# A hybrid decoder trunk: the state space scan by blocks of four tokens instead of token by token, with its tables made apart from the mixer

## The reference, cut to what matters

```python
for l in range(DEPTH):
    h = rmsnorm(x, norm_mix[l])
    u, sq, sk, sv, dq, dk, dv, gate_logits = split(h @ w_in[l])
    y_ssm = gelu(s5_ssm(u, ...)); glu_a, glu_b = split(y_ssm @ w_glu[l]); y_ssm = glu_a * sigmoid(glu_b)
    y_sb = stick_breaking_attention(sq, sk, sv)      # 8 heads of 64
    y_da = differential_attention(dq, dk, dv, lam)   # 4 heads, partial rotary, subln
    x = x + sum_n(sigmoid(gate_n) * (y_n @ w_branch[l, n])) @ w_out[l]
    x = x + cross_attention(rmsnorm(x), rmsnorm(mem)) @ w_xo[l]
    x = x + square(relu(rmsnorm(x) @ w_up[l])) @ w_down[l]
out = rmsnorm(x)

def s5_ssm(u, ...):            # 32 groups of 16 channels, 64 complex states in each
    lam_bar = exp(lam * exp(log_dt)); b_bar = (lam_bar - 1) / lam * b
    s[t] = lam_bar * s[t-1] + b_bar @ u[t]
    return real(c @ s[t]) + d * u[t]
```

## Time and profile before

| | |
|---|---|
| median of 3 runs | 1209.06 us (1208.31 to 1209.67) |
| profiled execution | 1207.81 us, span 1206.1 us, TensorE clock 0.935 |
| busy in the span | PE 1090.8, PEld 963.5, DVE 876.0, ACT 565.9, POOL 302.8 us |
| read from HBM | 168.11 MB |

### The profile page before, as it was taken

How to read it: one execution, slowest core, us unless ns; L and a number is a source line. 1 busy time by engine, 2 the same in 40 slices (tenths; PEclk the granted TensorE clock), 3 DMA queues, 4 the chain that set the end, 5 groups by cost and what they waited for, 6 DMA issues and landing times. The chain is left out here.

```text
span 1206.1 us, 18306 instructions
## 1 busy us (share of the span) xinstructions
PE 1090.8 (90%) x6855; PEld 963.5 (80%) x6855; DVE 876.0 (73%) x1236; ACT 565.9 (47%) x874; POOL 302.8 (25%) x362
## 2 busy tenths in 40 slices
PE   3997898879999799999979798988899987999996
PEld 3985677769989688998869566767699976998995
DVE  5769999986877475555567899999778756555553
ACT  4643433236565454444444443332475654544442
POOL 0496775510000000000008868653100000000000
PEclk7997988889999989999979988987899998999998
DMA  7652323323554445565646422422255543555550
GB/s 254 184 156 68 109 71 105 100 76 132 184 182 145 128 136 185 187 191 192 186 117 180 122 70 71 124 86 78 98 175 181 177 131 99 183 191 190 184 186 35
DMA packets 138076, 170.34 MB, mean 141 GB/s; under 512 B 18043, under 2 KB 96005, under 8 KB 137989
## 3 DMA queue, kind: packets, MB, share of 16 engines
q1 hardware_dynamic: 137572, 168.91, 44.3%
q10 hardware_dynamic: 416, 0.26, 0.1%
HBM read 168.11 MB, written 1.05 MB: 140 GB/s over the span
## 5 line engine op out<-in xcount | busy, mean ns | idle before, releaser
L1124 DVE TENSOR_TENSOR s_w_lo<-s_raw,s_w_hi 128x1024 fp32r<-128x1024 f32 x312 | 419.5, 1369 | 165.5 <-ACT s_w_hi L742 161.0
L742 ACT ACTIVATE s_w_hi<-s_raw 128x1024 fp32r<-128x1024 f32 x312 | 320.9, 1054 | 186.7 <-PE p_T L1586 114.6
L1584 PE MATMUL p_T<-s_hT_hi,s_w_hi 128*128 128x256 f32 x1152 | 341.9, 297 | 14.2 <-DVE s_hT_lo L1184 14.2
L1585 PE MATMUL p_T<-s_hT_lo,s_w_hi 128*128 128x256 f32 x1152 | 336.8, 292 | 0.0
L1586 PE MATMUL p_T<-s_hT_hi,s_w_lo 128*128 128x256 f32 x1152 | 336.4, 292 | 0.0
L1584 PEld LDWEIGHTS p_T<-s_hT_hi,s_w_hi 128*128 128x128 f32 x1152 | 233.0, 202 | 26.5 <-issue 26.0
L1585 PEld LDWEIGHTS p_T<-s_hT_lo,s_w_hi 128*128 128x128 f32 x1152 | 233.2, 202 | 0.5
L1586 PEld LDWEIGHTS p_T<-s_hT_hi,s_w_lo 128*128 128x128 f32 x1152 | 232.1, 201 | 0.0
L1584 PE MATMUL p_A<-s_w_hi,s_bT_hi 128*128 128x512 f32 x320 | 124.9, 390 | 2.4 <-DVE s_bT_lo L1124 2.4
L1585 PE MATMUL p_A<-s_w_lo,s_bT_hi 128*128 128x512 f32 x320 | 124.7, 390 | 0.0
L1586 PE MATMUL p_A<-s_w_hi,s_bT_lo 128*128 128x512 f32 x320 | 124.5, 389 | 0.0
(11 more groups left out here) (249 smaller groups left out, 1824.4 us busy)
## 6 DMA issues: line engine op xcount, KB each, us to landing
s_raw<-in_w_in SPq DMA_DIRECT2D x104, 512.0 KB, 3.6
s_raw<-in_w_up SPq DMA_DIRECT2D x64, 512.0 KB, 3.7
s_raw<-in_w_down SPq DMA_DIRECT2D x64, 512.0 KB, 3.6
s_raw<-in_w_branch SPq DMA_DIRECT2D x24, 512.0 KB, 3.6
s_raw<-in_w_out SPq DMA_DIRECT2D x16, 512.0 KB, 3.6
s_raw<-in_w_xkv SPq DMA_DIRECT2D x16, 512.0 KB, 3.5
s_raw<-in_ssm_w_glu SPq DMA_DIRECT2D x8, 512.0 KB, 3.5
s_raw<-in_w_xq SPq DMA_DIRECT2D x8, 512.0 KB, 3.5
```

The lines of the kernel that those rows point to most:

```text
L742: return nc.scalar.activation(o, i, f, **kw)
L1124: return V.tensor_tensor(o, i0, i1, op)
L1584: mm(o, lhi, rhi, start=first, stop=False, **kw)
L1585: mm(o, lhi, rlo, start=False, stop=False, **kw)
```

## The change

The scan goes over blocks of 4 tokens. With the input laid out by blocks (`uB`, filled by `blocks`), `bt` folds four tokens into one state update, `ct` reads the state at the block's start for four tokens, and a block Toeplitz matrix `kt` (with the skip term in it) gives what the four tokens do to each other. Per tile the scan has 64 places instead of 256, and there are four steps instead of eight. The tables are larger: `p_angle`, `p_cos` (ScalarE, VectorE), `tables` and `zero_b` (GpSimd: powers, a 64-place rotation table, zeroing), `p_cv`, `p_b0`, `p_bv` (VectorE), `p_ct`, `p_k`, `p_bt` (TensorE, emptied by ScalarE). Layer 0 makes them at units 0 to 6 and begins the scan at unit 7, layer 1's are made at units 50 to 70 of layer 0 and its scan begins at unit 8; `gelu` follows at unit 12 and 13. The rings shrink, the work on `mem` before layer 0 goes, and `mem` is loaded again in each layer.

```diff
-LO, HI = 10, 6
+LO, HI = 6, 4
...
+        after(u["angle"], "p_angle", tgt)
+        after(u["cos"], "p_cos", tgt)
+        after(u["ct"], "p_ct", tgt)
...
+        pre(0, dict(angle=0, cos=0, ct=1, cv=(1, 2), b0=3, bv=(3, 4), k=(4, 4), bt=(4, 5, 5, 6)))
+        first = 7
+        pre(1, dict(angle=up0 + 6, cos=up0 + 7, ct=up0 + 9, cv=(up0 + 11, up0 + 13), b0=up0 + 15,
+                    bv=(up0 + 16, up0 + 18), k=(up0 + 18, up0 + 20),
+                    bt=(up0 + 21, up0 + 22, up0 + 23, up0 + 24)))
+        after(up0 + 4, "p_spread", 1)
+        after(up0 + 5, "p_params", 1)
...
+    else:
+        first = 8
+    for kb in range(4):
+        after(first + kb, "ssm_in", kb)
+        after(first + 1 + kb, "ssm_out", kb)
+    after(first + 5, "gelu")
...
-    for i in range(SSM_STEPS):
-        after(7 + 2 * i, "ssm_in", i)
-        after(8 + 2 * i, "ssm_rot", i)
-        after(min(10 + 2 * i, 23), "ssm_out", i)
-    after(23, "gelu")
...
-    after(33, "memg")
+    after(33, "mem_turn", 0)
+    after(33, "mem_turn", 1)
+    after(34, "mem_turn", 2)
+    after(34, "mem_turn", 3)
```

The copy of u, run by VectorE for unit 0 and by ScalarE for unit 1, has 16 instructions:

```diff
+        def blocks(copy, b, key, st):
...
+            for q in range(4):
+                for j in range(BL):
+                    i = 8 * key[1] + q
+                    ins = copy(uB[32 * j:32 * j + 32, i:i + 5:4, :], src[32 * q:32 * q + 32, :, :, j])
```

GpSimd's program, in order, and the first waits of `p_cv` and `p_b0` on VectorE:

```diff
+                if l == 0:
+                    tables(st, 0, 0)
+                    zero_b(st, 0, 0)
...
+                if l + 1 < DEPTH:
+                    pool.wait_ge(*st.mine())
+                    tables(st, l + 1, l)
+                    zero_b(st, l + 1, l)
...
+                def p_cv(t, r):
+
+                    if r == 0:
+                        dve.wait_ge(*st.at(*freed(l, "X1", ("p_ct", t))))
+                        dve.wait_ge(*st.at(pow_ready, t + 1))
...
+                def p_b0(t):
+
+                    dve.wait_ge(*st.at(mat_landed, 6 * (t + 1)))
+                    dve.wait_ge(*st.at(pow_ready, t + 1))
+                    dve.wait_ge(*st.at(b_zeroed, t + 1))
```

The new scan step on VectorE (four tiles of 64 places; `io` is the bank, r the real and the imaginary part), and TensorE's two products:

```diff
+                    tt(v[:, :, :, 1:NB], io, turned(0)).then_inc(*st.mid())
+                    tt(t0[:, :, :, 1:NB], io, turned(1)).then_inc(*st.sig(*freed(l, b, s)))
                     dve.wait_ge(*st.mine())
...
+                        V.tensor_tensor_scan(vf, dect[:, sl, :].rearrange("p i m -> p (i m)"), vf, 0.0, ALU.mult, ALU.add)\
...
+                        for r in range(2):
+                            for q in range(4):
+                                c, i = r * T + q * NB, 4 * kb + q
+                                ins = mm(bank[b][:, c + 1:c + NB], bt[:, r, i, :], uB[:, i, 0:NB - 1],
+                                         start=True, stop=True)
...
                             for r in range(2):
...
+                                mm(bank[b][:, c:c + NB], ct[:, r, i, :], st_y[:, r, i * NB:i * NB + NB],
+                                   start=(r == 0), stop=False)
+                            ins = mm(bank[b][:, c:c + NB], kt[:, i, :], uB[:, i, :], start=False, stop=True)
```

More of the change, by code:

```diff
@@ L268, in stage_banks @@
         [["A0", "A1", "A3", "A2"][s[1]]] if s[0] == "xa_p" else [])
+NORMS = ["mix", "cross", "mlp"]
+NORM_SEQ = [(l, n) for l in range(DEPTH) for n in ("mix", "mem", "cross", "mlp") if n != "mem" or l == 0]
 KEYS = [None] * NU
@@ L424, in hybrid_trunk @@
         lo_made = signal("w_lo_made", NC)
-        lo_made_pool = signal("w_lo_made_pool", sum(2 * (pool_cols(u) > 0) for u in range(NU)))
         chunk_done = signal("chunk_done", NC)
[L427 to L433, removed]
+        prm_landed = counted("prm_landed", 9 * DEPTH, step=16)
@@ L559, in _ @@
                     load_chunk(l * NC + c)
[L560 to L570, removed]
@@ new lines, in zero_b @@
+            def zero_b(st, t, l):
+                pool.wait_ge(*st.at(h_ready, KD // 2 if l == t else 3 * KD // 2))
+                for h in range(2):
+                    rows, o = slice(STATES * h, STATES * h + STATES), GC * (1 - h)
+                    pool.wait_ge(*st.mine())
+                    nc.gpsimd.memset(bN0[rows, :, :, o:o + GC], 0.0).then_inc(*st.mid())
+                    for r in range(2):
+                        ins = nc.gpsimd.memset(bN[rows, r, :, :, o:o + GC], 0.0)
+                        ins.then_inc(*st.sig(b_zeroed, t + 1)) if h and r else ins.then_inc(*st.mid())
@@ new lines, in p_k @@
+                def p_k(s):
+                    t, n = s[1:]
+                    b = stage_banks(s)[0]
+                    act.wait_ge(*st.at(*full_at(l, b, s)))
+                    src = bank[b][:, :].rearrange("p (i c) -> p i c", c=P)
+                    for j in range(BL):
+                        rows = slice(32 * j, 32 * j + 32)
+                        ins = fn(kt[rows, 4 * n:4 * n + 4, 32 * j:P], src[0:32, :, 0:P - 32 * j])
+                        ins.then_inc(*st.sig(*freed(l, b, s))) if j == BL - 1 else ins.then_inc(*st.mid())
@@ L1568, in turn_rows @@
                 return ins
-            pe.wait_ge(mem_landed, 16)
-            for j, b in enumerate(TURN_BANKS):
-                turn_rows(b, j, xn).then_inc(pre_pe, 1)
-            pe.wait_ge(pre_dve, 4)
-            for t in range(NT):
-                ins = mm(bank["A1"][:, t * P:t * P + P], ones[:, :], dg[t], start=True, stop=True)
-            ins.then_inc(pre_pe, 1)
-            pe.wait_ge(pre_dve, 9)
             pe.wait_ge(x_landed, 16)
@@ L1682, in stage @@
-                        ins.then_inc(*st.sig(full["A1"]))
+                            ins = mm(bank[b][:, t * P:t * P + P], ones[:, :], dg[t], start=True, stop=True)
+                        ins.then_inc(*st.sig(full[b]))
                     elif kind == "turn_x":
                         for t in range(NT):
-                            pe.wait_ge(*st.at(*norm_input(s[1], s[2], t)))
+                            pe.wait_ge(*st.at(*norm_input(l, s[1], s[2], t)))
                         for j, b in enumerate(stage_banks(s)):
-                            pe.wait_ge(*st.at(*before(b, s)))
+                            pe.wait_ge(*st.at(*before(l, b, s)))
```

1087 lines of the change are left out of this document (590 added, 497 removed).

## The result

The changed kernel takes **1268.49 us** (median of 4 runs, 1266.31 to 1273.96) where the kernel before took 1208.68 beside it: a ratio of 1.0503, 95% interval 1.0468 to 1.0538. It is 5% slower. The forecast was 1212, in a range of 1178 to 1242. The profiled execution has a span of 1264.3 us, 58.2 more than before.

What follows compares the result with a forecast made beforehand. It took TensorE to bound the MLP and VectorE's late head chains, with lost clock, the mixers; terms -5 + 57 - 39 - 43 + 19 + 12 + 5 - 2 = +4 on 1207.8 gave 1212 us, range 1178 to 1242.

Steps and rivals of the forecast that it cites:

- Layer 0's tables: Layer 0's first units: waiting on one chain through GpSimd to p_k leaves TensorE idle about 25 us; +57 (45 to 68).
- Layer 1's tables in the MLP: Layer 0's MLP: TensorE's added table work of 17.5 us, the other engines' hidden in slack, plus a lump; +19.
- +1.5 for that (0 to +12): Layer 0's MLP: allowance for p_b0 at unit 61 waiting on GpSimd, 45 us behind the cosines.
- 41 to 55: GpSimd's chain from the cosines through tables and zero_b: estimated us before p_b0 may start, 46 taken.
- a rival at 0.14, with 1237: Layer 0's MLP: late b_zeroed holds VectorE before p_b0 with low parts behind; GpSimd at 55, +25, 1237; chance 0.14.
- mild at small sizes: GpSimd and VectorE contention, as argued for the rival of cheap narrow products and sufficient ring: 1188, chance 0.27.
- The mixers, -39 and -43: Units 6 to 25, layers 0 and 1: VectorE relieved, TensorE waits only for gelu and the last heads; bounds +-12 each.
- Smaller rings, +6 in each layer: After the mixers: preparation serves a unit one sooner, so units 35, 37 and 40 wait; bounds 0 to +10.
- a stall costs twice: TensorE: idle time is followed by half clock; after 4.17 us idle a product took 1.65 us instead of 0.91.
- Memory again: +2.7: Layer 0, the memory redone per layer: 16 transposes at 0.13 and a broadcast; +2.1 in layer 1.
- The start: Before unit 0: the memory's load, statistics and transposes go, so VectorE's run begins earlier; -5, bounds -3 to -8.
- The rival without a hole: Layer 0's first units: p_b0 ready by unit 4, 25 us less and more, 1180; chance 0.05.

Runs made afterwards that it cites:

- e1: The changed kernel with GpSimd's six memsets of the B tables placed ahead of its tables in both layers: 1219.55 us.
- e2: The changed kernel with layer 1's p_b0, p_bv, p_k and p_bt six units later in layer 0's MLP: 1242.59 us.
- e7: The changed kernel with SyncE issuing layer 1's 15 small loads, and waiting for the MLP's norm, four chunks later: 1267.18 us.
- e3: The changed kernel with each gelu half's 16 activations replaced by one of 128x512, without the token permutation: 1250.06 us.
- e4: The kernel before with rings of 6 and 4 chunks for 10 and 6, and preparation two chunks less ahead: 1227.78 us.
- e9: The changed kernel with layer 1's scan from unit 2 in place of unit 8: 1278.20 us.
- e10: Layer 1's scan from unit 2, against e5 with e7's edit and unit 35's chunks prepared ahead of the memory's work at unit 33: 1202.30 us.
- e5: e1 with one gelu activation per half into a scratch tile, and permuting copies later on VectorE and ScalarE: 1198.02 us.

## Why the prediction was wrong

It forecast +4 and got +60 (58.2 in the profile). Three terms fail, each on the side of what the change adds; they carry 26, 15 and 7 of the 54 by which the stages miss. Layer 0's tables are 5 more.

*Layer 1's tables in the MLP, +19, measured +45.4.* The 17.5 of TensorE's work was nearly right: without the waits it is about 20 (45.4 less 20.8 by e1 and e2, less 4.8 by e7's profile). What failed is "+1.5 for that (0 to +12)". The step before it was right in its mechanism and wrong in one number: GpSimd needs "41 to 55", taken from rows of 128x16 at 0.2 us, and took 64.9. I had it as a rival at 0.14, with 1237, and the mechanism is that rival's; it came on top of all other terms, and 10 us late became 22. Beside GpSimd's chain in the MLP, VectorE makes the low parts of a unit every 5.7 us or so. I let contention cost VectorE's low parts 1.1 us and gave GpSimd's operations 5 us in all; a 16-element operation goes from 0.2 to 0.8 to 1.2 us when it meets one, and some 75 of the 115 instructions in the chain are of that size. GpSimd's pairs of 16 elements in the changed kernel, the first beside VectorE's work and the second while VectorE stood:

```profile
551.73 2.35 POOL L673 TENSOR_TENSOR s_small<-s_small 128x16 f32<-128x16 f32 x2
...
577.56 0.39 POOL L673 TENSOR_TENSOR s_small<-s_small 128x16 f32<-128x16 f32 x2
```

The trace of the kernel before had the price already. The row I took (45.96 in the earlier trace rows) stands beside small operations of VectorE; 17 us later four operations of the same size meet two low parts and take 0.7 each:

```profile
63.06 2.83 POOL L625 TENSOR_TENSOR s_ptmp<-s_pw,s_small 128x16 f32<-128x16 f32 x4 [0.17 <-POOL s_small L625]
...
63.05 2.38 DVE L1124 TENSOR_TENSOR s_w_lo<-s_raw,s_w_hi 128x1024 fp32r<-128x1024 f32 x2
```

So "mild at small sizes" holds only where both engines' operations are small. And SyncE's loads, which I named and priced at nothing, are 4.8 in e7's profile.

*The mixers, -39 and -43, measured -32.2 and -35.2.* The steps about the engines hold: VectorE is far under TensorE (106 us in 188.6), the low parts are back at 2.35 a pair, the clock is 0.96, the heads' waits of the earlier trace rows are gone, and the narrow products cost what I took, 0.23 to 0.25 (my "256 0.5" stands in no row, but the result did not hang on it):

```profile
137.82 2.00 PE L1843 MATMUL p_A<-s_uB,s_bt 128*128 128x63 f32 x16
```

(two passes each). The term that failed is `gelu`: 32 activations at 0.28 were 0.41, and the evacuation is behind all of them. 7 of idle became 11.7, and 5 became 11.1. By e3 the small activations in place of two cost 12.5 and 10.4 with its half clock, for the 9 and 5 that I had: 9 of the 15 missing. Where the other 6 are stays open.

*Smaller rings, +6 in each layer.* In the kernel before, e4 shows the waits in the branches, as forecast, and a price of 9.8 and 9.5: I wrote at the top that a stall costs twice and then left the half clock out of this term. In the changed kernel only layer 0 misses (+16.9 for +8.7, with the memory). Layer 1, with the same rings and the memory's turns, takes +6.5 where I had +8.1: its wait at unit 35 is 0.2 us, where e4, with `memg` still in VectorE's order, has 3.5. What layer 0 has on top is the memory's statistics, 6.0 us at unit 35. So the step that failed is "Memory again: +2.7", for transposes and a broadcast: it counted TensorE's part of the moved work only, and not VectorE's place in its order.

*Layer 0's tables, +57, measured +62.3.* Cosines 12.4 us after unit 0 (12), unit 3 8.6 late (9), GpSimd 50.9 (46, bounds 41 to 55), the hole 32.5 (25), `p_k` 13.6 (14). The miss of 5 is GpSimd's chain again.

The start, -7, lies in its bounds; layer 1's first units are 1 longer and not 2 shorter. The rival without a hole was out by the order of GpSimd's program, and e1 shows that this order was the whole matter: changed, it leaves 5.8 us of the hole.

## What to carry to other kernels

When work moves to an engine that shares something with a busy one, price its *chain* as it would run there, beside that work, and not from rows where the other engine stands; then ask which signal the chain raises last, and who waits for it with something urgent behind. Order the program of a helper engine by who waits: what needs no input (here six memsets) goes first. Break up any block on an engine that also empties banks: 32 small activations stopped TensorE for 11 us in each layer, and the same permutation in pieces on two engines cost 1 to 3 us. Give every stall its clock as a term of its own.

## What was unexpected of the hardware

- A GpSimd operation of 128x16 took 0.2 us with VectorE idle and 0.8 to 1.2 beside its two-input operations; the same chain of 115 instructions took 50.9, 64.9 and 75.4 us with VectorE busy beside it for 14.7, 32.5 and 54.8 us. A low part of VectorE beside the small ones hardly grew (1.2 to 1.3 us, for 1.2).
- Behind a wait of 2.25 us the granted clock was 0.63 in the mean over 14 us in which TensorE was busy for 13.6, in e9 as in e10; behind the wait of 20.9 us one unit took 7.59 for 5.98. The length of the wait did not foretell its price.
- Fewer partitions saved nothing: ScalarE's copies of u, 32x128 from PSUM, took 0.27 us in the mean, one of 128x128 0.28. `gelu`'s of the same shape took 0.41, and e5's copies of it from SBUF 3.61/8 = 0.45. Both write every fourth element, the copies of u do not; whether that is the reason no run tests.
